# Gate projection of a hybrid block in four column groups of the array, with a product that adds the four partial sums

## What is computed

```
proj  = a @ w_in                    # a: 512 tokens x 1024 (256 context, 256 latent)
b, dt = proj[:, 2048:2056], proj[:, 2056:2064]     # 4 heads x 2 directions each
beta  = sigmoid(b)
g     = -exp(a_log) * softplus(dt + dt_bias)
# the delta rule: S_t = exp(g_t) S_{t-1} (I - beta_t k_t k_t^T) + beta_t k_t v_t^T
```

## Time and profile before

| | |
|---|---|
| time, median of 3 runs (lowest to highest) | 2289.66 us (2287.6 to 2290.04) |
| profiled execution: its own time, its span | 2289.95 us, 2288.1 us |
| TensorE busy, share of the span | 2221.1 us, 97% |
| ScalarE busy, VectorE busy | 51%, 71% |
| mean granted TensorE clock | 0.995 of full |
| the gate products (L1869): instructions, first to last start | 16, 60.5 to 67.0 us |

### The profile page before, as it was taken

How to read it: one execution, slowest core, us unless ns; L and a number is a source line. 1 busy time by engine, 2 the same in 40 slices (tenths; PEclk the granted TensorE clock), 3 DMA queues, 4 the chain that set the end, 5 groups by cost and what they waited for, 6 DMA issues and landing times.

```text
span 2288.1 us, 41418 instructions
## 1 busy us (share of the span) xinstructions
PE 2221.1 (97%) x17332; PEld 2045.9 (89%) x17332; DVE 1617.5 (71%) x2749; ACT 1156.7 (51%) x1937; POOL 150.9 (7%) x142
## 2 busy tenths in 40 slices
PE   7999999999999999999999999999999999999998
PEld 3665979998879999999999989997779999999998
DVE  4398667655977655798557787577988557799654
ACT  3425355443365446756345664345556345957343
POOL 0013000000000000000000000015630000000000
PEclk9999999999999999999999999999999999999999
DMA  8248054555244554414554425552024554514552
GB/s 365 74 198 318 25 215 167 186 185 201 93 166 166 185 185 167 182 56 178 182 182 161 147 93 203 184 221 74 19 94 184 184 184 169 183 54 166 185 184 74
DMA packets 50873, 368.46 MB, mean 161 GB/s; under 512 B 5632, under 2 KB 5888, under 8 KB 6528
## 3 DMA queue, kind: packets, MB, share of 16 engines
q1 hardware_dynamic: 50544, 363.72, 43.1%
q10 hardware_dynamic: 144, 2.10, 0.2%
HBM read 364.75 MB, written 1.05 MB: 160 GB/s over the span
## 4 chain that ended last, share of the span: by engine, by line
PE 81%; DVE 11%; ACT 5%; issue 2%; DMA 0%; SPq 0%; DVEq 0%; POOL 0%; ACTq 0%
PE psum L268 67%; DVE weight_rest L262 2%; PE psum L4515 1%; PE psum L3076 1%; PE psum L4516 1%; ACT weight_parts L226 1%; PE psum L4537 1%; PE psum L3710 1%; PE psum L2726 1%; DVE work L2028 1%; PE psum L4551 1%; DVE work L3540 1%; DVE spare L2516 0%; DVE work L2515 0%; DMA weight_ring<-stream_dram 0%
## 5 line engine op out<-in xcount | busy, mean ns | idle before, releaser
L268 PE MATMUL psum<-input_parts,weight_parts 128*128 128x256 f32 x5184 | 931.6, 283 | 6.4 <-DVE work L1495 1.8
L268 PEld LDWEIGHTS psum<-input_parts,weight_parts 128*128 128x128 f32 x5184 | 799.3, 189 | 11.6 <-issue 5.7
L268 PE MATMUL psum<-input_parts,weight_rest 128*128 128x256 f32 x2592 | 732.6, 283 | 0.0
L262 DVE TENSOR_TENSOR weight_rest<-weight_ring,weight_parts 128x1024 fp32r<-128x1024 f32 x528 | 619.9, 1220 | 149.3 <-ACT weight_parts L226 148.9
L226 ACT ACTIVATE weight_parts<-weight_ring 128x1024 fp32r<-128x1024 f32 x540 | 538.0, 1051 | 122.5 <-PE psum L268 121.7
L268 PEld LDWEIGHTS psum<-input_parts,weight_rest 128*128 128x128 f32 x2592 | 487.8, 188 | 0.0
L268 PE MATMUL psum<-hidden_parts,weight_parts 128*128 128x256 f32 x2496 | 450.8, 283 | 2.6 <-DVE weight_rest L262 1.3
L268 PEld LDWEIGHTS psum<-hidden_parts,weight_parts 128*128 128x128 f32 x2496 | 385.0, 189 | 5.9 <-issue 3.4
L268 PE MATMUL psum<-hidden_parts,weight_rest 128*128 128x256 f32 x1248 | 352.1, 282 | 0.0
L268 PEld LDWEIGHTS psum<-hidden_parts,weight_rest 128*128 128x128 f32 x1248 | 234.9, 188 | 0.0
L1479 ACT ACTIVATE work<-psum 128x256 f32<-128x256 f32 x118 | 45.3, 384 | 352.4 <-PE psum L268 350.0
(11 more groups left out here) (532 smaller groups left out, 2855.9 us busy)
## 6 DMA issues: line engine op xcount, KB each, us to landing
weight_ring<-stream_dram SPq DMA_DIRECT2D x340, 1024.0 KB, 4.8
constants<-constants_dram SPq DMA_DIRECT2D x1, 2304.0 KB, 17.1
work<-s_bc_dram ACTq DMA_DIRECT2D x1, 2048.0 KB, 9.7
work<-ctx_dram SPq DMA_DIRECT2D x1, 1024.0 KB, 5.3
residual<-x_dram SPq DMA_DIRECT2D x1, 1024.0 KB, 7.3
work<-first_dram SPq DMA_DIRECT2D x1, 1024.0 KB, 14.9
out_dram<-residual SPq DMA_DIRECT2D x4, 256.0 KB, 2.1
vectors<-vectors_dram SPq DMA_DIRECT2D x1, 486.5 KB, 14.3
```

Of the source, the lines that this page charges most:

```text
L262: ins = dve.tensor_tensor(self.rest[:, i % RING, cols], self.ring[:, i % RING, cols], self.parts[:, s % SPLITS, cols].bitcast(F32), ALU.su ...
L268: mm = pe.matmul(*args, **kw)
```

## The change

The 16 gate columns are packed together for each feature chunk, 8 of `dt` beside 8 of `b` (`hyb_gates_w`, the same 128 columns in all). `gate_strips` multiplies 32 columns at a time (16 of them belong to the chunk, the other 16 are whatever lies behind) and places the product of chunk c in column group c mod 4 of the array, so that it lands in 32 rows of the bank; chunks 4 to 7 add to chunks 0 to 3. The bank then holds four partial sums in rows 0, 32, 64 and 96 onwards. ScalarE copies the whole bank (128 x 512) to SBUF behind its square after chunk 4, and behind chunk 5 TensorE multiplies the copy with a constant matrix of 72 columns, which adds the four and puts `dt` in rows 0 to 7 and `b` in rows 64 to 71 of the same bank. `gate_exps` waits for that product. The constants grow by 72 columns (36 KB in the DMA that loads them), and a reserved piece of SBUF ahead of all buffers shrinks from 1024 to 64 bytes in each partition.

```diff
+GATE_ROWS = 72
-    ("hyb_a_log", 1), ("hyb_dt_bias", 1), ("hyb_g_w", KC * 8), ("hyb_beta_w", KC * 8),
+    ("hyb_a_log", 1), ("hyb_dt_bias", 1), ("hyb_gates_w", KC * 16),
...
-    ("time", T), ("future", 2 * P),
+    ("time", T), ("future", 2 * P), ("gate_sum", GATE_ROWS),
...
+def gate_strips(k, pe, out, name, x, ready=None):
+
+    for c in range(KC):
+        at = STRIP * (c % 4)
+        if ready:
+            pe.wait_ge(*ready[c])
+        mm = pe.matmul(out[at:at + STRIP, :], k.v(name, 16 * c, STRIP), x[:, c, :], start=(c < 4), stop=(c >= 4),
+                       tile_position=(0, at))
+    return mm
...
-        self.gate_taken, self.gate_exp = k.counter("gate_taken").events(2)
+        self.gate_copied, self.gate_taken, self.gate_exp = k.counter("gate_taken").events(3)
+        self.gate_strips = k.area(H_GATE + 2 * T2, T2)
...
+            if n == 5:
+                self.sum_gates(pe)
...
-        rows = KC * 8 + 8
-        w = self.k.v("hyb_g_w", 0, 2 * KC * 8)
-        for c in range(KC):
-            mm = pe.matmul(job.ap[0:rows, 0:T2], w[:, 8 * c:8 * c + rows], self.a[:, c, :],
-                           start=(c == 0), stop=(c == KC - 1))
-        mm.then_inc(job.full[0], 1)
+        gate_strips(self.k, pe, job.ap[:, 0:T2], "hyb_gates_w", self.a).then_inc(job.full[0], 1)
+
+    def sum_gates(self, pe):
+
+        pe.wait_ge(*self.gate_copied)
+        pe.matmul(self.gate_job.ap[0:GATE_ROWS, 0:T2], self.k.c("gate_sum"), self.gate_strips, start=True, stop=True)\
+          .then_inc(self.gate_summed[0], 1)
...
+            if n == 4:
+                act.wait_ge(*self.gate_job.full)
+                act.activation(self.gate_strips, self.gate_job.ap[:, 0:T2], ACT.Identity)\
+                   .then_inc(self.gate_copied[0], 1)
             if n == 5:
                 self.gate_exps(act)
...
-        act.wait_ge(*job.full)
+        act.wait_ge(*self.gate_summed)
...
-    nc = _bacc.Bacc("TRN2", target_bir_lowering=False, num_devices=1, dynamic_dma_scratch_size=1024)
+    nc = _bacc.Bacc("TRN2", target_bir_lowering=False, num_devices=1, dynamic_dma_scratch_size=64)
```

More of the change, by code:

```diff
@@ L1779, in setup @@
             if n == 4:
+                self.gate_summed = k.bank_full[k.jobs % BANKS]
                 self.gate_job = k.job(self.gate_taken)
+                self.gate_summed = self.gate_summed.event()
             for i in self.sums_after.get(n, ()):
@@ L4895, in small, with both @@
         return np.asarray(w).reshape(KC, P, 8).transpose(1, 0, 2).reshape(P, KC * 8)
+    def both(a, b):
+        return np.stack([a.reshape(P, KC, 8), b.reshape(P, KC, 8)], 2).reshape(P, KC * 16)
     def states(a):
@@ L4905, in pack_vectors @@
     v["hyb_a_log"], v["hyb_dt_bias"] = rows(i["hyb_a_log"]), rows(i["hyb_dt_bias"])
-    v["hyb_beta_w"], v["hyb_g_w"] = small(i["hyb_w_in"][0][:, 2048:2056]), small(i["hyb_w_in"][0][:, 2056:2064])
+    v["hyb_gates_w"] = both(small(i["hyb_w_in"][0][:, 2056:2064]), small(i["hyb_w_in"][0][:, 2048:2056]))
     v["hgrn_norm_w"] = chunks(i["hgrn_norm_w_2"])
@@ L4966, in pack_constants @@
     c["future"] = np.concatenate([np.where(t[:, None] <= t[None, :], 0.0, FUTURE), np.zeros((P, P))], 1)
+    c["gate_sum"] = np.zeros((P, GATE_ROWS))
+    for r in range(8):
+        c["gate_sum"][r::STRIP, r] = c["gate_sum"][8 + r::STRIP, 64 + r] = 1.0
     for name, size in CONSTANTS:
```

## The result

| | before | after |
|---|---|---|
| time, median of 5 runs each | 2289.66 us (2287.6 to 2291.8) | 2268.69 us (2266.12 to 2269.15) |
| ratio, 95% interval | | 0.9907 [0.9892, 0.9921] |
| span of the profiled execution | 2288.1 us | 2267.3 us |

The change gains 21.0 us. The forecast was 4.9 us and its range ended at 2282.8 us, so the result lies well outside. The engines' shares hardly move: TensorE is still busy for 97% of the span and carries 79% of the chain. Here is the page of the kernel after.

What follows compares the result with a forecast made beforehand. TensorE, busy 97% of the span, was taken as the bound, with ScalarE pacing the gates. Strips gain 4.87 us, copy and adding product cost 0: 2285.1 us profiled, 2284.8 median; 8-in-10 range 2282.8 to 2287.4.

Steps and rivals of the forecast that it cites:

- -4.87 + 0 + 0: Whole sum: TensorE gains 4.87 us at the gate strips; ScalarE's copy and the adding product cost 0, being hidden.
- Slower: the layout: Rival, chance 5%: moved buffer starts cost each matmul at most 0.43 ns; if all 17332 paid, 7.5 us, giving 2292.3.
- must keep 355.9 ns for three: Sign: 256-column products elsewhere keep 355.9 ns per three; if they lengthen, the layout is at fault.
- Strips: Gate products on TensorE: 16 strips, four abreast, take 2.00 us with entry and exit instead of 6.87, gaining 4.87.
- less overlap: Rival, chance 7%: gate strips overlap less at 512 columns; two abreast gains 3.15 us, giving 2286.5 us.
- one after the other: Rival, chance 3%: the strips' column groups run serially, TensorE is 0.28 us later at chunk 5, giving 2289.9 us.
- The copy: ScalarE's added 0.60 us bank read near 64.1 us, behind the square after chunk 4: hidden, 0.5 us to spare.
- The adding product: On TensorE behind chunk 5: two instructions, 0.86 us, hidden with 0.35 us to spare; uncovered, at most 1.06 us.
- Gate functions: Sign: ScalarE starts the gate functions at about 69.1 us, without waiting for the adding product.
- the turn: TensorE's return after the gate functions and VectorE's g: at about 75.2 instead of 80.05 us, 0.9 us idle before it.
- Given back later: Rival, chance 5%: a later wait, candidate the weight stream, takes the gain back; half gives 2287.2 us, all 2289.7.
- The clock: Spread belonging to every case: one stretch at the lower clock level more or less moves a run by 1.44 us.

Runs made afterwards that it cites:

- e1: Kernel before with only the changed kernel's buffer addresses (reserved block 64 bytes, 72 unused constant columns), gates as before: 2274.69 us, ratio 0.9935.
- e4: Kernel before with 72 unused constant columns and a reserved block of 736 bytes; weights 288 bytes lower, activations unmoved: 2276.39 us, ratio 0.9943.
- e7: Kernel before with weights 64 bytes lower and activations unmoved, by padding between them: 2249.22 us, ratio 0.9828.
- e2: Changed kernel with every buffer at its address of before, the adding matrix in its own buffer and load: 2283.06 us, ratio 0.9972 to before.
- e3: Kernel before with only the reserved block cut to 64 bytes, all buffers 960 bytes lower: 2289.66 us, ratio 0.9998.
- e5: Kernel before with all buffers 32 bytes lower (reserved block 992 bytes): 2289.26 us, ratio 1.0003.
- e6: Kernel before with weights 64 bytes lower and activations 32 lower, 32 bytes of padding between: 2274.97 us, ratio 0.9939.
- e9: Changed kernel with 32 bytes of padding behind the constants, distance remainder 64 by 128: 2237.0 us, ratio 0.979 to before.
- e8: Kernel before plus appended TensorE-only stretches of 96 fp32r products, own weights each, at varied operand offsets: 117.8 to 120.0 ns per product with activations moved.
- e11: Kernel before plus appended TensorE-only stretches of 96 fp32r products in the kernel's triples, at varied offsets: 116.7 to 120.0 ns with activations moved; 113.3 or 117.8, weights moved 64.
- e12: Kernel before plus appended TensorE-only stretches with alternating offsets, separating distances to own and next product's weights: 116.7 ns (0, 64), 118.3 (64, 0).

## Why the prediction was wrong

**The step that failed** is the sum, "-4.87 + 0 + 0": it holds no term for the buffers' new places. The forecast named them only as a rival, "Slower: the layout", and priced them at "at most" 0.43 ns for each matmul, upwards. The rival looked in the right place, a cost that hangs on where operands start. But its sign was the other, its size three times that price (1.31 ns for each of 12,960 products, 17.0 us, of which 15.7 became lead), and it hangs on the distance between two operands, not on the offset of one. e1 shows that it needs nothing of the gates, e4 to e7 that it is the distance. The terms that the sum does hold were right: the gates alone, e2, came out at 2283.06 us, inside the range.

**Why the rows misled.** The price came from one stretch of 256 columns, 355.9 ns for three, and one of 258 columns, 360.0. The kernel before also runs products of 256 columns at 360 ns for three (at 1108.92 us, shown above). So the 360.0 could as well be a slower rhythm as the two further columns, and the bound "at most what offsets cost" rested on two rows that the trace itself contradicts 700 us later. The same operation compared with itself in several stretches would have shown that its pace isn't one number, and that a change of it in either direction was open: a tenth of a nanosecond is worth 1.3 us here. The rule stated at the end, that products "must keep 355.9 ns for three" and would give the layout away "if they lengthen", had the right place to look at; they became shorter.

**What held.**
- Strips: 2.00 us with entry and exit were forecast. They take 1.85 to the start of the sums, and the four sums then 1.82 (62.27 to 64.09) against 1.72 before (67.38 to 69.10), so 1.95 in all. Four groups do run four abreast at 512 columns; "less overlap" and "one after the other" fall.
- The Trainium skill, page "TensorE: Matmul & The Clock Gate", section "Measured speedup vs the span model", has 3.07 times for four row tiles at 512 columns. This trace, with four column groups, has 6.87 / 1.85 = 3.7 with the entry in it, and the measurement decides.
- The copy: expected at about 64.1 us, hidden with 0.5 to spare; it started at 63.85, and 0.84 us stayed free.
- The adding product: hidden, as forecast. Gate functions at 68.85 (69.1 forecast), the turn at 75.05 (75.2), idle before it 0.88 (0.9).
- "Given back later" falls: the lead is 5.07 us at the first fp32r product, 234 us after the turn, and e2, where the pace stays as it was, ends 6.9 us earlier with an interval that holds 4.9.
- The clock played a small part at most: the profiled executions have 0.996 of full after and 0.995 before, and 0.001 of the span is 2.3 us.

## What to carry to other kernels

When an edit moves buffers, its layout is a change of its own: run the layout without the edit, and the edit with the old layout, before the gain is credited to either. Where one form of matmul fills the span, compare its start-to-start distance in several stretches and both traces first, since a nanosecond over 13,000 products outweighs a stage that was made almost four times as fast. A few bytes of padding between the two operands is an experiment that costs one line; here 32 bytes more, found only by trying, gave another 32 us by the medians.

## What the runs showed that was not expected

- The pace of fp32r products of 256 columns hangs on the distance between activations and weights: 119.3 to 119.4 ns mean at a remainder of 0 (before, e2, e3, e5), 118.0 to 118.3 at 32 (after, e1, e4, e6), 118.4 at 96, 115.7 and 114.6 at 64. In the bare stretches distances with one remainder differ, and so do the kernels' products with exchanged roles, so the remainder by 128 orders these kernels' means and is not a law.
- It comes in a few fixed rhythms (113.3, 116.7, 117.3, 117.8, 118.3, 118.7, 120.0 ns), entered at the start of a dense stretch and mostly kept to its end; one distance can show two. What picks the rhythm at the start stays open, and with it why e9's runs lie 27 us apart.
- The Trainium skill, page "TensorE: Matmul & The Clock Gate", section "Back-to-back issue gap", says that the spacing of pairs of load and product is set by both. The runs agree in so far as the weights' place moves the step as the activations' does (117.8 ns or less with either moved by 64 in e8 and e11); e12 points to the load of the next product and does not prove it. The same section's figure for a product alone gives 256 / 2.4 + 2.5 = 109.2 ns as an estimate; the lowest rhythm of any run is 113.3.
- Four column groups at 512 columns cost 1.85 us for 16 strips, entry included, against 6.87 us for 16 plain instructions.
